# Heads of the second group computed inside their own stream, the sample tile's top-k first, a sixth slot for u rows

## The chip, the cores and the metric

The kernel runs on one core of a Trainium2 chip. The metric is the device time of one launch in microseconds; lower is better. The engines are PE (TensorE, matrix products), DVE (VectorE), ACT (ScalarE), POOL (GpSimd, which here issues the gathers) and SP (SyncE, which issues the weight loads). 16 DMA engines serve the core.

## What is computed

Two layers of a decoder trunk for two request groups that share weights: a prompt of 512 rows and 8 sample sequences of 8 rows (64 rows). Cut to what matters here:

```python
x += MixerBlock(rmsnorm(x))        # w_in (1024 x 7168), short conv, spatial gate, w_a_out, w_b_out, w_mix_o
x += CrossAttn(rmsnorm(x), mem)    # 4 heads, 256 memory tokens (a cache of its own for each sample sequence)
h = rmsnorm(x)                     # PEER
q = h @ w_pq                       # 8 heads x 2 halves x 128
s = q @ sub_keys                   # per head two lists of 128 scores
s1, i1 = top_k(s[..., 0], 16); s2, i2 = top_k(s[..., 1], 16)
cand = s1[:, None] + s2[None, :]; top_s, pos = top_k(cand, 16)
idx = (i1 * 128 + i2)[pos]         # 8 x 16 = 128 experts for each row
g = softmax(top_s)
out = sum_e g_e * gelu(h . peer_u[idx_e]) * peer_v[idx_e]
```

Each expert row is 1024 float32. For 128 rows of x, one *pick* (one of the 128 expert places) needs a gather of 128 rows of `peer_u` and 128 rows of `peer_v`, 0.524 MB each.

## The kernel before

**Tiles, passes and steps.** The rows are five tiles: prompt tiles 0 to 3 of 128 rows and the sample tile 4 of 64 rows. They form two groups: tiles 0 and 1; tiles 2, 3 and 4. A *pass* p is one layer for one group; p = 0 and 2 are the first group, 1 and 3 the second. Each pass has a *trunk* (mixer, cross-attention, scores) and a *stream* (its picks). The sample tile has its heads folded to two halves of the partitions and needs 64 picks, so the streams have 256, 320, 256 and 320 picks: they begin at picks 0, 256, 576 and 832, and there are 1152 in all. The order of the whole program is counted in *steps*, one for each pick m: POOL issues the u gather of pick m and then the v gather of pick m - 8 (`LAG`), DVE forms the dot products of pick m, and the sum of pick m - 8 is added, either by DVE (`sum_up`) or by PE as a product with a diagonal matrix that ACT writes (`peer_to` of PE; the picks in `plan_sums`). A stretch of PE sums is closed by a `merge` on DVE.

**Rings.** u rows have `NU` = 5 slots and v rows `NV` = 5. POOL works in order: u(m) waits until the dot of m - `NU` is done, v(m) until the sum of m - `NV` is done. Weights come through three slots `W` of 2 MB, each reloaded by SP when PE has finished the unit in it.

**What runs beside what.** The trunk of pass p runs during the stream of pass p - 1. `places` gives each trunk job a step; PE starts no job before its step's sums, and ACT and DVE take a job's result only when they come to its step. Before the change the trunk of pass 1 stands at steps 40 to 200, then its queries and scores (`pq`, `sc`, eight heads) at 200 to 247, all ahead of its stream at 256; that of pass 3 at 586 to 776 and 776 to 823, ahead of 832. The trunk of pass 2 has its first part (`par` to `v`) at 266 to 336, the rest at 336 to 520 and the heads to 567.

**Top-k.** The first tile of a pass gets its top-k head group by head group (`top_group`, sizes 2, 2, 2, 1, 1 in passes 1 to 3 and 1, 1, 2, 2, 2 in pass 0), cut in nine pieces between which `breathe` lets the stream go on as far as the window of the group has steps. For the later tiles `top_k` does all heads at once inside the stream, in 18 pieces spread over `topk_window`. `turns_to` counts the finished ones, in the order in which POOL, ACT and DVE wait for them.

**Sums.** In pass 1's stream the first 72 picks are summed on PE, then DVE sums until the last 56 picks; in pass 3's stream two of three are summed on PE. In pass 3 the dots read the tile's rows from PSUM (`rows_in_psum`, filled by `copy_rows` on ACT), otherwise from the SBUF tile `T`.

```python
if p == 2 * DEPTH - 1:
    return step_base(p) + NSEL * (i - 1) + OVER, step_base(p) + NSEL * i - LATEST
if p % 2:
    return step_base(p) + (0, TILE1)[i - 1], step_base(p) + (TILE1, 2 * HEAD)[i - 1]
```

Of the kernel before, what the change touches and what calls it, by code (L numbers as in the profile page):

```python
# [23 lines left out]
P = 128  # L24
# [7 lines left out]
DEPTH, CW = 2, 3  # L32
# [10 lines left out]
GRP = 4  # L43
NU, NV = 5, 5
WRING = 4
# [7 lines left out]
OVER = 3  # L53
TILE1 = 54
LATEST = 20
SEGS = 9
DIAG_EARLY = 3
# [39 lines left out]
def topk_window(p, i):  # L97

    if p == 2 * DEPTH - 1:
        return step_base(p) + NSEL * (i - 1) + OVER, step_base(p) + NSEL * i - LATEST  # L100
    if p % 2:
        return step_base(p) + (0, TILE1)[i - 1], step_base(p) + (TILE1, 2 * HEAD)[i - 1]
    if p:
        return step_base(p) + OVER, step_base(p) + NSEL - LATEST
    return step_base(p) + FIRST, step_base(p) + FIRST + WIDE
# [5 lines left out]


def head_steps(p):

    return (FIRST + LAG, 2 * HEAD, 0, 0)[p]

# [67 lines left out]


def head_groups(p):

    sizes = (2, 2, 2, 1, 1) if p else (1, 1, 2, 2, 2)
    return [(sum(sizes[:k]), n) for k, n in enumerate(sizes)]
# [9 lines left out]
def places(p):  # L199
# [4 lines left out]
    if p == 0:  # L204
# [5 lines left out]
        return out  # L210
    begin, end = step_base(p - 1) + (FIRST if p == 1 else LAG + 2), step_base(p)
    if p % 2:
        stretches = [(0, late, begin, end - CLOSE)]
    else:
        stretches = [(0, early, begin, step_base(p - 1) + 2 * HEAD), (early, late, step_base(p - 1) + 2 * HEAD, end - CLOSE)]
    stretches.append((late, len(mine), end - CLOSE, end - OVER - 6))
    out = []
# [8 lines left out]
def plan_jobs():  # L226
# [7 lines left out]
    for p in range(2 * DEPTH):  # L234
# [3 lines left out]
        for k, (name, owner, width, cost) in enumerate(mine):  # L238
# [7 lines left out]
            else:  # L246
# [4 lines left out]
                summing = any(a <= place[k] + 2 and since <= b + 1 for a, b in held_by_sums) or name[1] in ("pq", "sc")  # L251
                top = 6 if held or summing else 8
                cursor += cursor % width
                if cursor + width > top:
                    cursor = 0
                at = cursor
# [64 lines left out]
def plan_sums():  # L321
# [10 lines left out]
    for p in range(2 * DEPTH):  # L332
# [8 lines left out]
        for i, (t, rows) in enumerate(GROUPS[p % 2]):  # L341
            end = at + tile_picks(rows)

            since = at + 4 if i else at
            share = 2 if i == len(GROUPS[p % 2]) - 1 else 3
            span(at, end, step_base(p) + end - b + LAG, lambda m: m % share and m >= since)
            at = end
# [3 lines left out]
def decoder_step(nc, A, O):  # L351
# [17 lines left out]
    with ExitStack() as ctx:  # L369
# [44 lines left out]
        pos = sb("pos", [P, PH, TOPK], U16)  # L414
        part_of = sb("part_of", [P, 2, PH, TOPK], U16)
        pair = sb("pair", [P, PH, 2, TOPK], U16)
        sel = sb("sel", [P, PH, TOPK])
        gsum = sb("gsum", [P, PH])
# [197 lines left out]
        def final_steps(t):  # L616

            last = step_base(2 * DEPTH - 1)
            if t < 2:
                return last + 2 * HEAD + 8 + 12 * t, last + 2 * HEAD + 12 + 12 * t  # L620
            end = last + sum(tile_picks(rows) for n, rows in GROUPS[1] if n <= t) + LAG
# [7 lines left out]
        def head_window(p, k):  # L629

            ends = [AHEAD[p, "sc", h + n - 1] for h, n in head_groups(p)] + [FIRST if p == 0 else step_base(p) - OVER]
            return ends[k], ends[k + 1]

        def turns_to(p, i, h=PH - 1):

            n = sum(PH + len(GROUPS[q % 2]) - 1 for q in range(p))
            return n + h + 1 if i == 0 else n + PH + i

# [457 lines left out]
        def _(act):  # L1096
# [41 lines left out]

            asides = [(topk_steps(p, i, topk_parts(p, i)[1]), gate_exp, (p, i)) for p in range(2 * DEPTH) for i in range(1, len(GROUPS[p % 2]))]
            asides += [(final_steps(t)[0], final_square, (t,)) for t in range(NTILE - 1)]  # L1140
            asides += [(step_base(2 * DEPTH - 1) + at, copy_rows, (i,)) for i, at in ((1, 16), (2, 2 * NSEL - LATEST + GRP))]
            asides.sort(key=lambda a: a[0])
# [60 lines left out]
            def trunk(p):  # L1203
# [120 lines left out]
                for h in range(PH):  # L1324
# [9 lines left out]
                    for k, (h0, some) in enumerate(head_groups(p)):  # L1334
                        if k and h == h0 + some - 1:
                            group_exps(p, k - 1)
                if p == 2 * DEPTH - 1:
                    copy_rows(0)
                k = len(head_groups(p)) - 1
# [15 lines left out]
        def _(dve):  # L1355
# [88 lines left out]

            asides, going = [(p, i) for p in range(2 * DEPTH) for i in range(1, len(GROUPS[p % 2]))], []

# [143 lines left out]
            def top_group(p, k):  # L1590
# [300 lines left out]
```

## Time and profile before

| | us |
|---|---|
| median of 3 runs | 4321.12 (4315.29 to 4326.33) |
| the profiled execution | 4322.15 |
| its span | 4320.3 |

| engine | busy us | share |
|---|---|---|
| PE | 3404.0 | 79% |
| DVE | 3008.0 | 70% |
| POOL | 2638.8 | 61% |
| ACT | 930.1 | 22% |

The profile has one execution. Its first u gather starts at 503 us, when pass 0 has its first expert numbers; from there a stretch of steps is found in the trace by counting u gathers. Busy shares are means over stages whose limits differ, so the stage's own row is read, not the whole. "DMA share" is the mean busy share of the 16 DMA engines; it reads up to 1.03 where they are full.

### The profile page before, as it was taken

To read this page: it belongs to the slowest core of one execution; us is meant where nothing else is said; L and a number is where in the kernel's file an instruction comes from. 1 tells how busy PE (TensorE), PEld (TensorE's weight loads), DVE (VectorE), ACT (ScalarE), POOL (GpSimd) and SP (SyncE) were. 2 spreads that over 40 slices of the span, in tenths; PEclk is the share of its full clock that TensorE was granted. 3 is DMA by queue.
4 is the path that set the end of the run, shared out by engine and by line. 5 is a ranking of instruction groups with operands and counts; after the bars stand their busy time and mean duration, and the time that the engine had idled before them with its cause. 6 is when DMAs were issued, how large, how long until landed. Compare 5 with 4: busy or idle time off the path is not lost.

```text
span 4320.3 us, 36550 instructions
## 1 busy us (share of the span) xinstructions
PE 3404.0 (79%) x11088; PEld 2044.9 (47%) x11088; DVE 3008.0 (70%) x5941; ACT 930.1 (22%) x2730; POOL 2638.8 (61%) x2318
## 2 busy tenths in 40 slices
PE   8999979998888778968756959998777866556655
PEld 6875645774645323756334525764544422222211
DVE  2101377967668876886878688987768877776676
ACT  1001231121322322112212321122312311221221
POOL 0000175665657677777667676676667677777775
PEclk9899999999989899979877989899888888888878
DMA  5335498989999999999999989999999899999998
GB/s 190 120 136 185 178 355 311 390 334 357 364 369 403 363 361 374 399 388 405 409 400 401 397 312 361 404 374 397 366 368 403 313 401 409 404 410 409 403 410 329
DMA packets 461419, 1518.69 MB, mean 352 GB/s; under 512 B 41124, under 2 KB 45540, under 8 KB 461224
## 3 DMA queue, kind: packets, MB, share of 16 engines
q0 software_dynamic: 331776, 1208.11, 72.3%
q1 hardware_dynamic: 129448, 308.25, 19.0%
q8 instruction: 90, 1.47, 0.1%
q14 instruction: 105, 0.86, 0.1%
HBM read 1508.97 MB, written 7.23 MB: 351 GB/s over the span
## 4 chain that ended last, share of the span: by engine, by line
DMA 20%; POOL 19%; PE 12%; DVE 11%; issue 9%; ACT 1%; DVEq 0%; ACTq 0%
DMA vrow<-in_peer_v_dram,idx 15%; POOL urow L801 10%; POOL vrow L801 9%; PE ps L858 5%; DMA urow<-in_peer_u_dram,idx 4%; PE ps L883 4%; PE ps L902 3%; DVE X L1412 3%; DVE urow L1396 2%; DVE ps L1412 1%; DVE RB L1515 0%; DVE RB L1743 0%; PE ps L1084 0%; DVE T L1662 0%; DVE RB L1511 0%
## 5 line engine op out<-in xcount | busy, mean ns | idle before, releaser
L801 POOL DMA_INDIRECT urow<-in_peer_u_dram,idx x1152 | 1343.0, 1166 | 1192.5 <-DVE idx L1521 499.9
L801 POOL DMA_INDIRECT vrow<-in_peer_v_dram,idx x1152 | 1293.6, 1123 | 468.6 <-issue 305.6
L858 PE MATMUL ps<-vrow,diag 128*128 128x512 f32 x1804 | 993.0, 689 | 481.7 <-DMA vrow<-in_peer_v_dram,idx 460.2
L883 PE MATMUL ps<-RH,W 128*128 128x256 f32 (+1 forms) x4608 | 1169.4, 415 | 155.0 <-DVE RH L1676 61.1
L1396 DVE CUSTOM_DVE_ANT_0 urow<-urow,T 128x1024 f32<-128x1024 f32 x832 | 1015.8, 1223 | 312.5 <-DMA urow<-in_peer_u_dram,idx 280.5
L883 PEld LDWEIGHTS ps<-RH,W 128*128 128x128 f32 x4608 | 896.4, 195 | 429.9 <-DVE RH L1676 62.1
L858 PEld LDWEIGHTS ps<-vrow,diag 128*128 128x128 f32 x1804 | 360.8, 214 | 1067.2 <-issue 925.1
L1412 DVE SCALAR_TENSOR_TENSOR X<-vrow,wts,X 128x1024 f32<-128x1024 f32 x580 | 745.9, 1286 | 144.0 <-issue 130.3
L1396 DVE CUSTOM_DVE_ANT_0 urow<-urow,ps 128x1024 f32<-128x1024 f32 x320 | 389.1, 1220 | 211.9 <-DMA urow<-in_peer_u_dram,idx 207.2
L1165 ACT ACTIVATE gel<-dots 128x4 f32<-128x4 f32 x288 | 59.1, 205 | 2135.2 <-DVE dots L1396 2072.7
L902 PE MATMUL ps<-W,RB 128*128 128x512 f32 (+1 forms) x576 | 251.7, 597 | 7.1 <-ACT RB L1201 3.0
L883 PE MATMUL ps<-RB,W 128*128 128x256 f32 (+1 forms) x1024 | 251.5, 406 | 2.9 <-DVE RV L1777 1.5
L1167 ACT ACTIVATE wts<-gel,gate 128x1 f32<-128x1 f32 x1152 | 245.0, 283 | 9.3
L883 PEld LDWEIGHTS ps<-RB,W 128*128 128x128 f32 x1024 | 194.4, 190 | 57.3 <-DVE RV L1777 1.9
L902 PE MATMUL ps<-W,RV 128*128 128x512 f32 (+1 forms) x320 | 143.4, 608 | 42.7 <-DVE RV L1777 42.7
L1180 ACT ACTIVATE diag<-ident,wts 128x128 f32<-128x128 f32 x451 | 157.3, 390 | 89.7 <-PE ps L858 88.9
L902 PEld LDWEIGHTS ps<-W,RB 128*128 128x128 f32 (+1 forms) x576 | 105.6, 185 | 150.0 <-issue 140.3
L1412 DVE SCALAR_TENSOR_TENSOR ps<-vrow,wts,ps 128x1024 f32<-128x1024 f32 x115 | 148.2, 1289 | 15.1 <-DMA vrow<-in_peer_v_dram,idx 4.3
L902 PE MATMUL ps<-W,RH 128*128 128x512 f32 (+1 forms) x320 | 144.6, 605 | 15.6 <-DVE RH L1676 15.6
L1201 ACT ACTIVATE RB<-ps 128x256 f32<-128x256 f32 (+3 forms) x134 | 53.8, 419 | 312.5 <-PE ps L883 260.8
L902 PEld LDWEIGHTS ps<-W,RV 128*128 128x128 f32 (+1 forms) x320 | 58.1, 184 | 126.4 <-issue 81.9
L1201 ACT ACTIVATE RV<-ps 128x256 f32<-128x256 f32 (+3 forms) x106 | 48.8, 465 | 283.2 <-PE ps L883 267.8
(240 smaller groups left out, 2305.4 us busy)
## 6 DMA issues: line engine op xcount, KB each, us to landing
W<-in_w_in_dram SPq DMA_DIRECT2D x56, 2048.0 KB, 17.8
W<-in_w_pq_dram SPq DMA_DIRECT2D x16, 2048.0 KB, 19.1
urow<-in_peer_u_dram,idx POOLq DMA_INDIRECT x1152, 9.2
vrow<-in_peer_v_dram,idx POOLq DMA_INDIRECT x1152, 9.2
W<-in_w_a_out_dram SPq DMA_DIRECT2D x8, 2048.0 KB, 18.1
W<-in_w_b_out_dram SPq DMA_DIRECT2D x8, 2048.0 KB, 18.9
W<-in_w_mix_o_dram SPq DMA_DIRECT2D x8, 2048.0 KB, 14.5
W<-in_w_xq_dram SPq DMA_DIRECT2D x8, 2048.0 KB, 15.4
```

Source lines behind the costliest of these rows:

```text
L801: return pool.indirect_dma_start(ring[:, slot, :], None, table, bass.IndirectOffsetOnAxis(ap=idx[:, q % TSLOT, e:e + 1], axis=0))
L858: o = pe.matmul(ps[:, bank + b, :], diag[:, pe_turn[m] % NDIAG, :], vrow[:, m % NV, b * 512:(b + 1) * 512], start=m in pe_first, stop=m in ...
L883: m = pe.matmul(pf(name), slot(u)[:, k, c % BLK * P:c % BLK * P + P], src[:, k, 0:ncols(name[0] % 2)], start=(k == 0), stop=(k == KC - 1))
L902: m = pe.matmul(ps[0:rows, BANK[p, kind, i] + a, :], src[:, k, i * P:i * P + rows], row_slot((p, kind, n))[:, k % 4, a * 512:(a + 1) * 512 ...
L1165: ch.link(act.activation(gel[:, :], dots[:, at, :], ACT.Gelu_apprx_tanh))
L1167: w = act.activation(wts[:, at, j:j + 1], gel[:, j:j + 1], ACT.Copy, scale=gate[:, q % TSLOT, e + j:e + j + 1])
L1180: act.activation(diag[:, pe_turn[m] % NDIAG, :], ident[:, :], ACT.Copy, scale=wts[:, m // GRP % WRING, m % GRP:m % GRP + 1]).then_inc(diag ...
L1201: act.activation(out, in_, func).then_inc(act_evac, 1)
L1396: dve.tensor_tensor_reduce(urow[:, m % NU, :], urow[:, m % NU, :], rows, 1.0, 0.0, ALU.mult, ALU.add, dots[:, n % WRING, m % GRP:m % GRP + ...
L1412: dve.scalar_tensor_tensor(out=out, in0=vrow[:, m % NV, :], scalar=wts[:, m // GRP % WRING, m % GRP:m % GRP + 1], in1=base, op0=ALU.mult, ...
```

## The change

Seven things are changed together.

1. The u ring has six slots. To make room, `part_of` and `sel` are no longer tiles of their own but lie in `m16`.
2. In passes 1 and 3 (`carries`) the eight heads of the first tile are scored at steps -26, -14, -6, 2, 12, 22, 33 and 44 from the stream's begin (`CARRIED`), so five of them inside the stream that uses them, in groups 1, 1, 2, 2, 2. The trunk ahead of them ends at step 227 and 803 instead of 200 and 776.
3. All 128 picks of the first tile of these passes are summed on PE.
4. The later tiles' top-k of pass 1 stand at steps 322 to 350 (the sample tile, now first) and 350 to 378 (tile 3's rows); before at 256 to 310 and 310 to 336 in the other order. In pass 3 tile 3's top-k stands at 898 to 952 instead of 835 to 940.
5. The trunk of pass 2 begins at step 321; its first part ends at 350, the rest at 520 as before.
6. A head group's gates are normalised (`weigh_group`) after the first piece of the next group instead of after its last.
7. In pass 3 trunk jobs after step 818 leave PSUM banks 0 and 1 free, and the copies of rows for the dots, and the final norms of tiles 0 and 1, are placed anew.

```diff
-NU, NV = 5, 5
+NU, NV = 6, 5
-TILE1 = 54
+SAMPLE = 94
+CARRIED = (-26, -14, -6, 2, 12, 22, 33, 44)
+CARRY = 64
 def topk_window(p, i):
     if p == 2 * DEPTH - 1:
-        return step_base(p) + NSEL * (i - 1) + OVER, step_base(p) + NSEL * i - LATEST
+        return step_base(p) + (CARRY + 2 if i == 1 else NSEL * (i - 1) + OVER), step_base(p) + NSEL * i - (8 if i == 1 else LATEST)
     if p % 2:
-        return step_base(p) + (0, TILE1)[i - 1], step_base(p) + (TILE1, 2 * HEAD)[i - 1]
+        return step_base(p) + (SAMPLE, CARRY + 2)[i - 1], step_base(p) + (NSEL - 6, SAMPLE)[i - 1]
+def later_tiles(p):
+    return (2, 1) if p == 1 else tuple(range(1, len(GROUPS[p % 2])))
 def head_steps(p):
-    return (FIRST + LAG, 2 * HEAD, 0, 0)[p]
+    return (FIRST + LAG, NSEL + LAG, 0, NSEL + LAG)[p]
+def carries(p):
+    return p % 2 == 1
 def head_groups(p):
-    sizes = (2, 2, 2, 1, 1) if p else (1, 1, 2, 2, 2)
+    sizes = (1, 1, 2, 2, 2) if p == 0 or carries(p) else (2, 2, 2, 1, 1)
 # places
-    begin, end = step_base(p - 1) + (FIRST if p == 1 else LAG + 2), step_base(p)
+    begin, end = step_base(p - 1) + (FIRST if p == 1 else CARRY + 1 if p % 2 == 0 else LAG + 2), step_base(p)
     if p % 2:
-        stretches = [(0, late, begin, end - CLOSE)]
+        stretches = [(0, late, begin, end + CARRIED[0] - OVER if carries(p) else end - CLOSE)]
     else:
-        stretches = [(0, early, begin, step_base(p - 1) + 2 * HEAD), (early, late, step_base(p - 1) + 2 * HEAD, end - CLOSE)]
-    stretches.append((late, len(mine), end - CLOSE, end - OVER - 6))
+        stretches = [(0, early, begin, step_base(p - 1) + SAMPLE), (early, late, step_base(p - 1) + SAMPLE, end - CLOSE)]
+    if carries(p):
+        first = late
+        for h in range(PH):
+            after = [k for k, j in enumerate(mine) if j[0] == ("sc", h)][0] + 1
+            stretches.append((first, after, end + (CARRIED[h - 1] if h else CARRIED[0] - OVER), end + CARRIED[h]))
+            first = after
+    else:
+        stretches.append((late, len(mine), end - CLOSE, end - OVER - 6))
 # plan_sums, pass 3
-            span(at, end, step_base(p) + end - b + LAG, lambda m: m % share and m >= since)
+            span(at, end, step_base(p) + end - b + LAG, lambda m: m < b + head or m % share and m >= since)
 # top_group
                 each(lists, lambda a: dve.max_index(i16[:, a, 0:8], m16[:, a, 0:8], part[a]))
                 breathe()
+                if k:
+                    weigh_group(p, k - 1)
...
                 expert_ids(marks, h, n, idx[:, kept, where], layer_of(p)).then_inc(idx_done, n)
                 breathe()
-                if k:
-                    weigh_group(p, k - 1)
```

How the instructions move is shown at two places. The first is PE where the trunk of pass 2 comes to its first blocks of `w_in` (steps 337 and 351). A sum of one pick is `ps<-vrow,diag 128x512 x2`; a trunk job is `ps<-RH,W 128x256 x8`. Before:

```order
L858 MATMUL ps<-vrow,diag 128x512 x6
L902 MATMUL ps<-W,RH 128x512 x10
L858 MATMUL ps<-vrow,diag 128x512 x28
L883 MATMUL ps<-RH,W 128x256 x32
L914 MATMUL ps<-GV,ident 128x128 x16
L883 MATMUL ps<-RH,W 128x256 x224
```

And now:

```order
L923 MATMUL ps<-W,RH 128x512 x10
L879 MATMUL ps<-vrow,diag 128x512 x12
L904 MATMUL ps<-RH,W 128x256 x8
L879 MATMUL ps<-vrow,diag 128x512 x2
L904 MATMUL ps<-RH,W 128x256 x8
L879 MATMUL ps<-vrow,diag 128x512 x4
L904 MATMUL ps<-RH,W 128x256 x8
L879 MATMUL ps<-vrow,diag 128x512 x2
L904 MATMUL ps<-RH,W 128x256 x8
```

Before, PE had these 32 jobs to itself while DVE summed; now one or two sums of tile 2's picks stand behind every job until step 392.

The second place is DVE in a late head group of pass 3. Dots are `urow,dots<-urow,...`; MAX, MAX_INDEX and MATCH_REPLACE are the top-k. Before, one of the single-head groups ahead of step 832:

```order
L1614 MAX m<-RB 128x8 x2
L1615 MAX_INDEX i<-m,RB 128x8 x2
L1396 ISA urow,dots<-urow,T 128x1024
L1396 ISA dots 128x1
L1617 MATCH_REPLACE RB<-m,RB 128x128 x2
L1618 MAX m<-RB 128x8 x2
L1620 MAX_INDEX i<-m,RB 128x8 x2
L1481 TENSOR_TENSOR RB<-m 128x64
L1484 TENSOR_TENSOR RB<-m 128x48
L1396 ISA urow,dots<-urow,T 128x1024
```

And now, a group of two heads inside the stream:

```order
L1633 MAX m<-RB 128x8 x4
L1634 MAX_INDEX i<-m,RB 128x8 x4
L1415 ISA urow,dots<-urow,ps 128x1024
L1415 ISA dots 128x1
L1415 ISA urow,dots<-urow,ps 128x1024
L1415 ISA dots 128x1
L1605 RECIPROCAL ginv<-gsum 128x2
L1607 TENSOR_TENSOR gate<-gate,ginv 128x32
L1638 MATCH_REPLACE RB<-m,RB 128x128 x4
L1639 MAX m<-RB 128x8 x4
L1415 ISA urow,dots<-urow,ps 128x1024
```

Two or three dots now stand between pieces of a group where one or none stood, and the rows of the dot come from PSUM.

## Rows read from the trace of the kernel before

**Rows 1.** Section 2 and the DMA total of the profile's page.
```profile
GB/s 190 120 136 185 178 355 311 390 334 357 364 369 403 363 361 374 399 388 405 409 400 401 397 312 361 404 374 397 366 368 403 313 401 409 404 410 409 403 410 329
DMA packets 461419, 1518.69 MB, mean 352 GB/s; under 512 B 41124, under 2 KB 45540, under 8 KB 461224
```

**Rows 2.** Busy time by stretch: start:end, length, engines (instructions), clock, DMA share, GB/s.
```profile
core 0: us, PE busy (x) PEld busy (x) DVE busy (x) ACT busy (x) POOL busy (x), PEclk, DMA share, GB/s
626.00:891.00 265.00, 258.30 (x885) 164.37 (x884) 226.82 (x540) 45.47 (x128) 159.12 (x129) 0.92 0.91 335
891.00:1377.00 486.00, 420.97 (x1581) 266.25 (x1580) 342.86 (x495) 123.11 (x307) 306.69 (x246) 0.93 0.97 372
1377.00:1476.00 99.00, 83.28 (x265) 46.52 (x264) 85.09 (x284) 32.26 (x98) 65.96 (x60) 0.94 0.98 375
1476.00:1603.00 127.00, 92.64 (x203) 35.92 (x202) 92.75 (x296) 33.87 (x113) 100.17 (x89) 0.94 0.98 362
1603.00:1760.00 157.00, 137.12 (x390) 71.84 (x389) 116.50 (x266) 35.67 (x108) 117.50 (x101) 0.95 0.99 376
1760.00:1903.00 143.00, 105.34 (x429) 85.85 (x427) 119.64 (x173) 14.69 (x67) 110.29 (x84) 0.83 1.03 403
1903.00:2521.00 618.00, 444.74 (x1573) 298.90 (x1574) 480.15 (x846) 152.31 (x432) 436.29 (x368) 0.86 1.02 397
2521.00:2635.00 114.00, 75.09 (x196) 32.04 (x195) 86.61 (x180) 22.10 (x67) 89.56 (x66) 0.85 0.83 297
2635.00:3048.00 413.00, 376.34 (x1326) 252.99 (x1325) 357.76 (x642) 77.49 (x204) 278.24 (x220) 0.90 1.00 386
3048.00:3352.00 304.00, 237.74 (x939) 149.49 (x938) 225.45 (x334) 79.32 (x214) 201.07 (x169) 0.89 0.99 385
3352.00:3453.00 101.00, 88.03 (x275) 48.86 (x274) 86.86 (x292) 35.28 (x106) 68.67 (x61) 0.88 0.88 311
3453.00:3577.00 124.00, 76.55 (x131) 26.67 (x130) 91.94 (x212) 26.05 (x101) 93.91 (x97) 0.88 1.02 400
...
503.00:4320.00 3817.00, 2928.39 (x9236) 1693.61 (x9234) 2932.08 (x5771) 870.68 (x2615) 2636.59 (x2304) 0.89 0.98 379
```

**Rows 3.** Three of the same stretches, u gathers on POOL alone: their count gives the steps.
```profile
626.00:891.00 265.00, 82.68 (x65) 0.92 0.91 335
...
1760.00:1903.00 143.00, 57.26 (x42) 0.83 1.03 403
...
2635.00:3048.00 413.00, 151.49 (x110) 0.90 1.00 386
```

**Rows 4.** Stretches again, the sums on PE alone (four instructions a pick): PE, PEld, clock, DMA.
```profile
1300.00:1377.00 77.00, 19.76 (x42) 7.76 (x43) 0.93 1.03 401
...
1476.00:1603.00 127.00, 86.83 (x170) 31.60 (x169) 0.94 0.98 362
...
3453.00:3577.00 124.00, 76.55 (x131) 26.67 (x130) 0.88 1.02 400
```

**Rows 5.** Groups of POOL from 1476 to 1603 us: count, busy, mean ns, idle before.
```profile
L801 POOL DMA_INDIRECT vrow<-in_peer_v_dram,idx x44 | 54.6, 1240 | 13.4 <-issue 7.6 <-PE ps L858 5.8
L801 POOL DMA_INDIRECT urow<-in_peer_u_dram,idx x45 | 46.4, 1031 | 13.7 <-issue 13.7
```

**Rows 6.** POOL's waits (total, times, longest) from 626 to 1300 us, then from 1903 to 2521 us.
```profile
POOL urow L801 <- DVE dots L1396: 167.0, 60, 10.6
...
POOL urow L801 <- DVE dots L1396: 46.6, 25, 6.8
```

**Rows 7.** GB/s in 40 slices from 3395 to 3453 us.
```profile
GB/s 325 271 384 398 418 393 401 407 410 415 396 412 379 136 268 136 381 373 297 314 342 288 381 277 381 133 3 82 308 237 102 17 206 322 206 184 220 345 376 297
```

**Rows 8.** DVE on tile `KV`, tile 3's top-k, from 1476 to 1663 us.
```profile
1476.00:1663.00 187.00, 40.82 (x202) 0.94 0.97 359
```

**Rows 9.** Section 5 of the page: a dot and a sum on DVE.
```profile
L1396 DVE CUSTOM_DVE_ANT_0 urow<-urow,T 128x1024 f32<-128x1024 f32 x832 | 1015.8, 1223 | 312.5 <-DMA urow<-in_peer_u_dram,idx 280.5
...
L1412 DVE SCALAR_TENSOR_TENSOR X<-vrow,wts,X 128x1024 f32<-128x1024 f32 x580 | 745.9, 1286 | 144.0 <-issue 130.3
```

More of the change, by code:

```diff
@@ L252, in plan_jobs @@
                 top = 6 if held or summing else 8
+                low = 2 if p == 2 * DEPTH - 1 and place[k] > step_base(p) + CARRIED[1] else 0
                 cursor += cursor % width
-                if cursor + width > top:
-                    cursor = 0
+                if cursor < low or cursor + width > top:
+                    cursor = low
                 at = cursor
@@ L414, in decoder_step @@
         pos = sb("pos", [P, PH, TOPK], U16)
-        part_of = sb("part_of", [P, 2, PH, TOPK], U16)
         pair = sb("pair", [P, PH, 2, TOPK], U16)
-        sel = sb("sel", [P, PH, TOPK])
         gsum = sb("gsum", [P, PH])
@@ L442, in decoder_step @@
         qT, oT = F1, F2
+        spent = m16[:, :, :].rearrange("p (h i) n -> p h i n", i=2)
+        sel = spent[:, :, 1, :]
+        part_of = m16[:, :, :].bitcast(U16).rearrange("p (h i) n -> p h i n", i=2)[:, :, 0, :].rearrange("p h (j n) -> p h j n", j=2)
         S = [RB[:, 0:2 * DM], KV[:, 0:2 * DM], RB[:, 2 * DM:3 * DM]]
@@ L619, in final_steps @@
             if t < 2:
-                return last + 2 * HEAD + 8 + 12 * t, last + 2 * HEAD + 12 + 12 * t
+                return last + NSEL - 4 + 8 * t, last + NSEL + 8 * t
             end = last + sum(tile_picks(rows) for n, rows in GROUPS[1] if n <= t) + LAG
@@ L629, in head_window @@
         def head_window(p, k):
-            ends = [AHEAD[p, "sc", h + n - 1] for h, n in head_groups(p)] + [FIRST if p == 0 else step_base(p) - OVER]
+            ends = [AHEAD[p, "sc", h + n - 1] for h, n in head_groups(p)] + [FIRST if p == 0 else step_base(p) + CARRY if carries(p) else step_base(p) - OVER]
             return ends[k], ends[k + 1]
@@ L636, in turns_to @@
             n = sum(PH + len(GROUPS[q % 2]) - 1 for q in range(p))
-            return n + h + 1 if i == 0 else n + PH + i
+            return n + h + 1 if i == 0 else n + PH + later_tiles(p).index(i) + 1
         def sum_step(m):
@@ L1137, in group_exps @@
                     head_exp(p, h)
-            asides = [(topk_steps(p, i, topk_parts(p, i)[1]), gate_exp, (p, i)) for p in range(2 * DEPTH) for i in range(1, len(GROUPS[p % 2]))]
+            asides = [(topk_steps(p, i, topk_parts(p, i)[1]), gate_exp, (p, i)) for p in range(2 * DEPTH) for i in later_tiles(p)]
             asides += [(final_steps(t)[0], final_square, (t,)) for t in range(NTILE - 1)]
-            asides += [(step_base(2 * DEPTH - 1) + at, copy_rows, (i,)) for i, at in ((1, 16), (2, 2 * NSEL - LATEST + GRP))]
+            asides += [(step_base(2 * DEPTH - 1) + at, copy_rows, (i,)) for i, at in ((0, -8), (1, CARRY + 8), (2, 2 * NSEL - LATEST + GRP))]
             asides.sort(key=lambda a: a[0])
@@ L1336, in trunk @@
                             group_exps(p, k - 1)
-                if p == 2 * DEPTH - 1:
-                    copy_rows(0)
                 k = len(head_groups(p)) - 1
@@ L1443, in final_tile @@
                                          in1=last_g[0:rows, :], op0=ALU.mult, op1=ALU.mult).then_inc(y_done, 1)
-            asides, going = [(p, i) for p in range(2 * DEPTH) for i in range(1, len(GROUPS[p % 2]))], []
+            asides, going = [(p, i) for p in range(2 * DEPTH) for i in later_tiles(p)], []
             def aside_to(n):
@@ L1490, in split_places @@
                 place = pos[:, h:h + nh, :]
-                by_wide, by_narrow = part_of[:, 0, h:h + nh, :], part_of[:, 1, h:h + nh, :]
+                by_wide, by_narrow = part_of[:, h:h + nh, 0, :], part_of[:, h:h + nh, 1, :]
                 row, col = pair[:, h:h + nh, 0, :], pair[:, h:h + nh, 1, :]
```

## The prediction

> **What bounds the kernel now.** I read the slices of the page first [rows 1]. After about the fifth slice the DMA engines are nearly full: the stream that no trunk disturbs holds 403 to 410 GB/s, and I take 409 GB/s as what this core can draw. Then I split the span by steps [rows 2], counting u gathers [rows 3]. From the first gather at 503 us to the end are 3817 us at 379 GB/s, so 1447 MB. At 409 GB/s they need 3537 us. The change moves no byte less, so **280 us is all that it can win**, and the question is in which stretches this loss lies. Loss is the length less GB/s times length over 409:
>
> - steps 0 to 40: 11 of 123, in the slices of the page.
> - steps 40 to 104 (626 to 891 us): 265 - 217 = 48. PE is busy 258 of 265 us and DVE 227.
> - steps 104 to 227 (to 1377): 486 - 442 = 44.
> - steps 227 to 256 (to 1476): 99 - 91 = 8.
> - steps 256 to 350 (to 1760): 284 - 257 = 27. There POOL hardly waits; its gathers last 1.03 and 1.24 us and 0.3 us lie between two [rows 5], so a step costs POOL 2.8 to 2.9 us, and hardly a weight is loaded that could use what is left of the DMA engines.
> - steps 350 to 576 (to 2521): 761 - 741 = 20.
> - steps 576 to 608 (to 2635): 114 - 83 = 31, the same picture.
> - steps 608 to 718 and 718 to 802 (to 3352): 23 and 18.
> - steps 802 to 832 (to 3453): 101 - 77 = 24. The fine slices fall to 3 and 17 GB/s [rows 7]: single-head groups with one to six steps to spread over.
> - the rest: 3 to step 880, and some 24 behind it, most of it the drain at the end.
>
> So the DMA engines bound the kernel, except where PE, DVE and POOL together can't feed them.
>
> **The change part by part.** One pick moves 1.05 MB, so 2.56 us at 409 GB/s. The sum is made against the profiled execution (4322.15 us; the median of the runs shown is 4321.12, 1 us less).
>
> *Steps 40 to 104.* The trunk ahead of the heads is spread over 187 steps instead of 160, so these 64 steps hold 34% of it instead of 40%. Of PE's 258 us, about 20 are the last ten sums of pass 0's first 40 picks at 1.9 us [rows 4]; the other 238 shrink to about 204, 224 with the sums. DVE keeps its dots, sums and the top-k of tile 1 and falls to about 219. The DMA engines need 217 less a seventh of 22 MB of weights (8 us), 209. With the margin that such a balance has now (265 over 258, with DVE at 227) I take 245: **-20**, bounds -35 and -5.
>
> *Steps 104 to 227.* They hold 66% of that trunk, where before they held 60% and the first half of the queries. The bytes stay (442 us), PE goes from 421 to about 410, DVE from 343 to 349. Nothing is removed; what goes is the cluster of queries, heads and their sums at the end and the density of the attention part, where DVE stands behind PE's jobs in order and POOL behind DVE: 167 us of waits for dots from 626 to 1300 [rows 6]. I take a loss of 19 instead of 44: **-25**, bounds -40 and 0.
>
> *Steps 227 to 256.* Three heads instead of six, two weight units (4 MB, 10 us) later: 99 to 90, **-9**, bounds -15 and 0.
>
> *Steps 256 to 350.* Five heads come in: 10 query jobs, about 45 us of PE with their scores. PE's sums cost 19.8 us for 10.5 picks to 86.8 us for 42.5, 1.9 to 2.0 us each [rows 4]; heads and sums together are 2.9 us a step over 44 steps, no more than POOL's 2.8 to 2.9. The 4 MB of weights fit in what the DMA engines have left. DVE loses the whole top-k of tile 3 and gains the heads. What is late next is POOL, as before: **0**, bounds -10 and +10.
>
> *Steps 350 to 392.* Here the change costs. Before, these 42 steps took 143 us, PE busy 105 of them without a sum [rows 2]. Now the trunk of pass 2 has 170 steps instead of 184 (105 becomes 113) and 42 sums are added. At 1.9 us these are 80: 193 us of PE against 143. The row's clock is 0.83 and rises to 0.95 and more where PE has no pause, so part of the 113 shrinks, down to 98; the DVE sums that PE takes over (1.29 us each [rows 9]) were not the limit. 178 to 193 against 143: **+40**, bounds +20 and +57. The moved weights come in behind: **+11**. The top-k of tile 3 in 28 steps is 41 us on DVE [rows 8] beside 34 of dots (28 at 1.22 us [rows 9]) and some 10 of trunk (119.6 us in the row of 42 steps, less 42 dots and 43 sums at 1.29 us), under PE's 28 x 4.4. It ends at 378, six steps ahead of its first gather, and may hold POOL for a few microseconds.
>
> *Steps 392 to 576 and 576 to 608.* Trunk 8% denser where the DMA engines are full (397 GB/s) and PE is idle a quarter: 0. The begin of pass 3's trunk lies as before: 0.
>
> *Steps 608 to 718.* Pass 3's trunk is spread over 217 steps instead of 190. The jobs that filled 608 to 701 now reach to 718: 17 steps more of picks for the same PE work (about 326 of the 376 us), DVE 347, the DMA engines 370. I take 388 for 413: **-25**, bounds -35 and -5. *Steps 718 to 802*: no step is freed, 0. *Steps 802 to 832*: three groups with ten-step windows instead of five in 36 steps; POOL at 2.9 and some weights give 92 for 101: **-9**, bounds -20 and 0.
>
> *Steps 832 to 880.* Five heads (45 us of PE) join the stream, and all picks are summed on PE, 48 at 1.9 to 2.3 us [rows 4]. 136 us of PE for 124 before, where the DMA engines were full: **+12**, bounds +3 and +30. Behind it PE has room for every sum.
>
> *The sixth u slot.* POOL works in order and v keeps five slots. v(n-8) waits for the sum of n-13, which DVE makes right behind dot n-5. So where DVE sums, the sixth slot gives one dot (1.2 us) of slack, not a step; where PE sums it gives a whole gather. Most waits for dots lie where the DMA engines are full (46.6 us from 1903 to 2521 [rows 6], at 397 GB/s) and are worth nothing. **-10**, bounds -30 and 0. The earlier gates, the aliased tiles and the moved copies: 0, since ACT is idle three quarters of the time and the gates come more than ten steps ahead of their picks.
>
> Sum: -20 - 25 - 9 + 0 + 40 + 11 - 25 - 9 + 12 - 10 = **-35 us, 4287 us**.
>
> One rule speaks against all of it. The rows show 403 to 410 GB/s for hundreds of microseconds. The Trainium skill, page DMA: Bandwidth & Descriptors, section Specifications, gives about 358 GB/s as the limit of HBM for one core. By it the stretches at 372 to 410 GB/s would be at or over the limit already and the sum would be near 0, at 4322 us. The trace does not agree: the mean after the first gather is 379. I give that rule no chance of its own.
>
> **The rivals.**
>
> *The jobs' own chain, not their density, sets steps 104 to 227 and 608 to 718.* Each trunk job waits for an evacuation and that for DVE's or ACT's place in the order; if this takes its time however many steps lie between, both -25 become -5, and the sum is +5: **4327 us**, no change. For it: PE is busy only 87% of 891 to 1377. Against it: spread jobs leave more steps between them for dots, and DVE's waits there cost gathers.
>
> *PE becomes the wall in the second streams (slower).* The 98 more picks on PE, beside trunk jobs, at the dear end of each row: 57 for 40 in steps 350 to 392, 7 for 0 ahead of it (2.04 us a sum), 36 for 12 from 832 (2.34 us a sum), and no use of the slot since v slots stay taken while PE is late: +58, **4345 us**. It decides as soon as a sum beside a trunk job costs over 2 us, because then the step is over 4.6 us where the DMA engines need 3.5. For it: 2.04 and 2.34 us are rows. Against it: these contain waits for rows that have not landed, which go when PE is late; PE's 19.8 us for 10.5 sums lie in a stretch at 401 GB/s.
>
> *Slack is what was missing.* If one gather more in the ring and looser heads let POOL run through the bursts, the slot gives 30 and PE's place costs 20: -75, **4247 us**. For it: POOL waited 60 times from 626 to 1300 us, 2.8 us on average, about one step. Against it: the v ring.
>
> *The slot does nothing*, the v ring alone decides: 4297 us, inside the forecast.
>
> **How the numbers follow.** Forecast with the idle slot in it 0.46, chain 0.20, PE wall 0.12, slack 0.22. A measurement of this kernel can tell about 0.3% or 13 us from no change. Faster: 0.22 + 0.46 (less 0.04 for its upper edge) + a bit of the chain, 0.68; slower: 0.12; same: 0.20. The range reaches from 4235, a little beyond the slack case, to 4332, beyond the chain case; it leaves out most of the PE wall and what lies below.
>
> **What would show it.** Steps 40 to 104 in about 245 us and 104 to 227 in about 461; 350 to 392 in about 183 instead of 143, PE full and the DMA share under 0.9; no slices under 100 GB/s ahead of step 832; 832 to 880 in about 136. u waits for dots fall, v waits for PE rise. The forecast is wrong if 104 to 227 stays at 486, if PE's stretch from 350 lasts 200 or only 150, or if a new wait of POOL for expert numbers appears at steps 288 to 384.

## The result: 0.36% slower, and where the 13 us lie

| | us |
|---|---|
| changed kernel, median of 14 runs | 4337.52 (4332.21 to 4347.30) |
| kernel before, 14 runs beside them | 4325.22 (4315.29 to 4334.43) |
| ratio | 1.0036, 95% interval 1.0028 to 1.0044 |
| span of the profiled execution, before and after | 4320.3 and 4333.3 |

The forecast was 4287 us with a range of 4235 to 4332. The change is slower, by a little, where it was called faster.

The page of the changed kernel, mean GB/s in 40 slices and the busy times:

```profile
PE 3518.1 (81%) x11480; PEld 2098.7 (48%) x11480; DVE 2888.1 (67%) x5843; ACT 973.2 (22%) x2833; POOL 2589.2 (60%) x2318
GB/s 186 126 134 183 187 359 359 384 361 402 376 374 304 374 371 358 358 342 403 400 408 402 406 312 363 391 385 406 376 358 342 369 387 409 396 411 409 409 408 330
```

Against [rows 1] the slices from the sixth to the twelfth are better in all but one (384 against 390 in the eighth). Then 304 stands where 403 stood, three slices around 1.8 ms have fallen (from 374, 399 and 388 to 358, 358 and 342), and near 3.3 ms 403 has become 342. DVE works 120 us less than before, PE 114 us more: the work moved as planned.

The same stretches as [rows 2], cut again by counting u gathers, for the changed kernel:

```profile
core 0: us, PE busy (x) PEld busy (x) DVE busy (x) ACT busy (x) POOL busy (x), PEclk, DMA share, GB/s
622.00:863.00 241.00, 227.13 (x793) 142.64 (x792) 221.68 (x528) 38.47 (x121) 147.00 (x128) 0.95 0.98 366
863.00:1234.00 371.00, 308.35 (x1163) 205.98 (x1164) 282.80 (x373) 100.23 (x235) 248.19 (x194) 0.89 0.98 376
1234.00:1343.00 109.00, 99.78 (x316) 48.58 (x316) 53.87 (x71) 19.12 (x52) 56.13 (x53) 0.94 0.88 332
1343.00:1449.00 106.00, 89.42 (x286) 51.81 (x287) 62.40 (x150) 27.07 (x89) 66.38 (x60) 0.94 0.95 362
1449.00:1735.00 286.00, 239.03 (x625) 111.50 (x624) 185.67 (x526) 86.00 (x266) 206.97 (x188) 0.97 0.97 363
1735.00:1907.00 172.00, 170.71 (x639) 118.50 (x638) 112.51 (x349) 34.86 (x112) 90.81 (x85) 1.00 0.95 352
...
2644.00:3035.00 391.00, 345.09 (x1207) 235.04 (x1206) 344.76 (x627) 71.35 (x193) 274.25 (x221) 0.90 1.02 394
3035.00:3255.00 220.00, 142.57 (x595) 93.88 (x594) 170.49 (x217) 56.74 (x148) 149.88 (x118) 0.82 0.95 367
3255.00:3363.00 108.00, 92.18 (x282) 43.96 (x281) 53.54 (x70) 20.05 (x57) 56.81 (x51) 0.92 0.88 342
3363.00:3461.00 98.00, 91.95 (x297) 53.26 (x296) 63.98 (x151) 27.93 (x90) 65.16 (x61) 0.96 0.96 368
3461.00:3589.00 128.00, 118.71 (x353) 61.38 (x352) 87.74 (x246) 42.88 (x136) 93.06 (x96) 1.00 1.01 388
```

Put side by side, in us; "e1" is the first experiment below:

| steps | before | forecast | changed | e1 |
|---|---|---|---|---|
| 0 to 40 | 123 | 123 | 119 | 119 |
| 40 to 104 | 265 | 245 | 241 | 242 |
| 104 to 201 | 409 | | 371 | 373 |
| 201 to 227 | 77 | | **109** | 89 |
| 104 to 227 together | 486 | 461 | 480 | 462 |
| 227 to 256 | 99 | 90 | 106 | 93 |
| 256 to 350 | 284 | 284 | 286 | 287 |
| 350 to 392 | 143 | 183 to 194 | 172 | 172 |
| 392 to 608 | 732 | 732 | 737 | 736 |
| 608 to 718 | 413 | 388 | 391 | 390 |
| 718 to 777 | 227 | | 220 | 220 |
| 777 to 802 | 77 | | **108** | 87 |
| 718 to 802 together | 304 | 304 | 328 | 307 |
| 802 to 832 | 101 | 92 | 98 | 98 |
| 832 to 880 | 124 | 136 | 128 | 127 |
| 880 to the end | 743 | 743 | 744 | 743 |

The gains of the spread trunk are there: 24 us in steps 40 to 104, 38 in 104 to 201 and 22 in 608 to 718. They are eaten by three places: steps 201 to 227 and 777 to 802, 32 and 31 us longer and the same place in two passes, which the forecast did not have; and steps 350 to 392, 29 us longer, which it had.

What happens in the first of them can be read from PE's instructions in order of time, in the changed kernel. `L923` from `W,RB` is the xo product (the attention's output projection), `L879` are sums, four instructions each:

```profile
1272.97 6.32 PE L923 MATMUL ps<-W,RB 128*128 128x512 f32 x8 [0.88 <-ACT RB L1222]
1280.23 1.95 PE L879 MATMUL ps<-vrow,diag 128*128 128x512 f32 x4 [0.94 <-DMA vrow<-in_peer_v_dram,idx]
1282.02 3.60 PE L923 MATMUL ps<-W,RB 128*128 128x512 f32 x8
1285.45 1.88 PE L879 MATMUL ps<-vrow,diag 128*128 128x512 f32 x4
...
1310.17 1.88 PE L879 MATMUL ps<-vrow,diag 128*128 128x512 f32 x4
1311.89 17.47 PE L923 MATMUL ps<-W,RB 128*128 128x512 f32 x40
1329.29 5.42 PE L879 MATMUL ps<-vrow,diag 128*128 128x512 f32 x12
```

POOL's waits in this stretch (total, times, longest) are:

```profile
POOL vrow L822 <- PE ps L879: 31.4, 7, 14.6
POOL vrow L822 <- DVE X L1431: 15.0, 5, 6.2
```

The xo product takes 42 us of PE where it stands alone (e1 below). It fell on steps 185 to 195 before, and now falls on 209 to 221. The span of PE sums that closes pass 0's stream begins at pick 201, so at step 209, in both kernels; PE makes three of four sums there, DVE the fourth. Before, the product had ended when PE began to sum; now PE sums while it makes the product, at first one sum for every 3.6 to 7.2 us of product and at the end none for 17.5 us. The v slots stay full, and POOL, which works in order, then issues neither v nor u gathers. Of its 31.4 us of waits for PE the block of 17.5 us accounts for one of 14.6; six shorter ones make the other 16.8.

PE is also simply full there. From its first sum to the three sums behind the block it has no pause, while the DMA share is 0.75:

```profile
1280.00:1334.50 54.50, 54.27 (x124) 21.43 (x125) 21.60 (x30) 10.13 (x30) 19.46 (x20) 1.00 0.75 278
```

The product over its 12 steps is 3.5 us a step, and three of four sums at 1.88 us add 1.4: about 4.9 us a step (an estimate), where a pick needs 2.56 us of the DMA engines. In the second stretch (3255 to 3363 us) it is not quite the same: PE stands still for 8.28 us ahead of its first sum, for a v row that has not landed, with most of the product behind that sum in its queue.

### The profile page after: what moved, and what is told of

Read it like the earlier page. It is cut to its first block, busy times and chain, and to the rows that moved or that the text cites. A ratio compares the mean times of both kernels' runs of the same rounds, so it can differ in the third digit from the quotient of the medians.

```text
span 4333.3 us, 37457 instructions
## 1 busy us (share of the span) xinstructions
PE 3518.1 (81%) x11480; PEld 2098.7 (48%) x11480; DVE 2888.1 (67%) x5843; ACT 973.2 (22%) x2833; POOL 2589.2 (60%) x2318
## 4 chain that ended last, share of the span: by engine, by line
PE 38%; DMA 22%; POOL 18%; DVE 11%; issue 8%; ACT 1%; SPq 0%; DVEq 0%; ACTq 0%; POOLq 0%
DMA vrow<-in_peer_v_dram,idx 17%; PE ps L904 17%; PE ps L879 10%; POOL vrow L822 10%; PE ps L923 9%; POOL urow L822 8%; DMA urow<-in_peer_u_dram,idx 4%; DVE X L1431 3%; DVE urow L1415 2%; PE ps L893 1%; PE ps L1105 1%; PE ps L1068 0%; DMA RH<-in_sg_w_dram 0%; DVE KV L1530 0%; DVE ps L1431 0%
## 5 line engine op out<-in xcount | busy, mean ns | idle before, releaser
L822 POOL DMA_INDIRECT vrow<-in_peer_v_dram,idx x1152 | 1328.2, 1153 | 856.8 <-DVE X L1431 319.4
L822 POOL DMA_INDIRECT urow<-in_peer_u_dram,idx x1152 | 1258.8, 1093 | 866.9 <-DVE idx L1540 499.6
L879 PE MATMUL ps<-vrow,diag 128*128 128x512 f32 x2196 | 1116.6, 644 | 396.0 <-DMA vrow<-in_peer_v_dram,idx 363.4
L879 PEld LDWEIGHTS ps<-vrow,diag 128*128 128x128 f32 x2196 | 416.4, 202 | 1020.3 <-issue 872.2
L1431 DVE SCALAR_TENSOR_TENSOR X<-vrow,wts,X 128x1024 f32<-128x1024 f32 x524 | 673.0, 1284 | 152.7 <-issue 129.5
L923 PE MATMUL ps<-W,RB 128*128 128x512 f32 (+1 forms) x576 | 257.6, 606 | 8.4 <-DVE RB L1813 4.4
L1201 ACT ACTIVATE diag<-ident,wts 128x128 f32<-128x128 f32 x549 | 198.2, 392 | 248.4 <-PE ps L879 247.3
L923 PE MATMUL ps<-W,RV 128*128 128x512 f32 (+1 forms) x320 | 144.4, 612 | 54.3 <-DVE RV L1796 54.3
L923 PEld LDWEIGHTS ps<-W,RB 128*128 128x128 f32 (+1 forms) x576 | 107.0, 188 | 155.0 <-issue 144.0
L923 PE MATMUL ps<-W,RH 128*128 128x512 f32 (+1 forms) x320 | 143.0, 600 | 19.5 <-DVE RH L1695 19.5
L923 PEld LDWEIGHTS ps<-W,RV 128*128 128x128 f32 (+1 forms) x320 | 58.4, 185 | 138.6 <-issue 82.5
L923 PEld LDWEIGHTS ps<-W,RH 128*128 128x128 f32 (+1 forms) x320 | 57.2, 181 | 101.0 <-issue 80.2
L1431 DVE SCALAR_TENSOR_TENSOR ps<-vrow,wts,ps 128x1024 f32<-128x1024 f32 x75 | 96.6, 1288 | 10.0 <-DMA vrow<-in_peer_v_dram,idx 4.1
```

The source lines that it names most:

```text
L822: return pool.indirect_dma_start(ring[:, slot, :], None, table, bass.IndirectOffsetOnAxis(ap=idx[:, q % TSLOT, e:e + 1], axis=0))
L879: o = pe.matmul(ps[:, bank + b, :], diag[:, pe_turn[m] % NDIAG, :], vrow[:, m % NV, b * 512:(b + 1) * 512], start=m in pe_first, stop=m in ...
L923: m = pe.matmul(ps[0:rows, BANK[p, kind, i] + a, :], src[:, k, i * P:i * P + rows], row_slot((p, kind, n))[:, k % 4, a * 512:(a + 1) * 512 ...
L1201: act.activation(diag[:, pe_turn[m] % NDIAG, :], ident[:, :], ACT.Copy, scale=wts[:, m // GRP % WRING, m % GRP:m % GRP + 1]).then_inc(diag ...
L1431: dve.scalar_tensor_tensor(out=out, in0=vrow[:, m % NV, :], scalar=wts[:, m // GRP % WRING, m % GRP:m % GRP + 1], in1=base, op0=ALU.mult, ...
```

## Theory and rivals for the experiments

A: the closing PE sums now stand beside the xo product in PE's queue. That can cost in two ways, and no run here keeps one and removes the other: the order (sums held behind product, the 17.5 us block) and the load (sums and product together are more than PE can do in these steps). B: attention and xo take their time wherever they lie, and only the place moved. C: the rings (a sixth u slot that gives nothing, or harms). For 350 to 392: PE's sums against DVE's load. The first four kernels ran on one chip with 13 runs of the kernel before (4320.94 us), the next three on a second (19 runs, 4324.71 us), the last two on a third; so ratios to before are compared, and stretches.

## e1: the closing PE sums begin behind the xo product

```diff
+TAIL = 32
 # plan_sums
-            span(b + n - CLOSE, b + n, ...)
+            close = CLOSE if p % 2 else TAIL
+            span(b + n - close, b + n, ...)
```

> The changed kernel, but the PE sums that close pass 0's and pass 2's streams begin at the last 32 picks (225 and 801) instead of the last 56 (201 and 777). Theory A: the time was lost in steps 201 to 227 and 777 to 802 (109 and 108 us against 78 and 77 before), because the xo product, which PE now makes at steps 209 to 221, stands in PE's order ahead of sums, so v slots stay full and POOL waits for v. Then DVE sums there free the slots: 201 to 227 falls from 109 to 80 to 90 us, 777 to 802 from 108 to 80 to 90, the whole to 4280 to 4305. Rival B: these steps are longer because attention and xo now fall into them, whoever sums: 201 to 227 stays over 100 us and the time within 10 us of 4337. Rival C: it was DVE's lost slack from another place, the ring of six: same as B here.

Measured: 4282.20 us, ratio 0.9899 (0.9874 to 0.9924). Against the changed kernel's 1.0036 that is 1.4% or 59 us from one number (55 by the medians, 52 by the two profiled spans). Steps 201 to 227, 227 to 256 and 777 to 802:

```profile
1239.00:1328.00 89.00, 78.81 (x265) 39.56 (x264) 62.94 (x79) 14.91 (x38) 57.40 (x52) 0.92 1.01 396
1328.00:1421.00 93.00, 78.25 (x264) 48.16 (x265) 70.22 (x153) 25.02 (x83) 68.38 (x58) 0.93 1.02 398
...
3226.00:3313.00 87.00, 72.12 (x240) 36.00 (x239) 63.23 (x78) 15.97 (x43) 58.33 (x51) 0.91 1.03 407
```

PE makes the product in one piece, and POOL's waits are short ones for DVE (PE's product, then the waits of 1239 to 1328 us):

```profile
1277.75 42.21 PE L925 MATMUL ps<-W,RB 128*128 128x512 f32 x94
...
POOL vrow L824 <- DVE X L1433: 18.1, 8, 4.0
```

The edit covers 24 picks in each pass; six of them DVE summed already, so DVE takes 18 sums more. With DVE at 54 of 109 us in the changed kernel it had the room. The DMA share rises from 0.88 to 1.01. A holds and B falls: attention and xo lie where they lay. By the table every stretch but these three is the changed kernel's to 2 us. That 227 to 256 falls from 106 to 93 is probably the lateness that it had inherited; seven of the 18 moved sums fall into it by the count of instructions.

PE's busy time falls with the length, from 99.78 to 78.81 us while the stretch goes from 109 to 89, so e1 shows that sums beside the product cost the time, and not whether it is their order or PE's load.

## e2: the same loss made in the kernel before

```diff
+TAIL = 86
-            span(b + n - CLOSE, b + n, ...)
+            close = CLOSE if p % 2 else TAIL
+            span(b + n - close, b + n, ...)
```

> The kernel before, but its closing PE sums of passes 0 and 2 begin 30 picks earlier (picks 170 and 746), so that they are on PE while it makes the xo product at steps 185 to 195 and 758 to 770. Theory A: the same loss appears in the old kernel, 15 to 30 us in each of the two passes, with v waits for PE of over 10 us beside the xo product: 4350 to 4385. Rival B: no difference beyond 10 us.

Measured: 4360.37 us, ratio 1.0084 (1.0062 to 1.0107), 36 us slower. Steps 178 to 201 and 756 to 777, first in the kernel before and then in e2:

```profile
1211.00:1300.00 89.00, 81.52 (x286) 42.45 (x284) 59.17 (x72) 15.94 (x39) 49.25 (x48) 0.93 1.02 397
...
3195.00:3275.00 80.00, 68.13 (x238) 34.86 (x236) 56.17 (x67) 16.84 (x40) 45.73 (x42) 0.94 1.03 406
```

```profile
1207.00:1313.00 106.00, 102.00 (x326) 48.73 (x324) 41.45 (x58) 20.43 (x54) 50.72 (x46) 0.98 0.83 317
...
3211.00:3306.00 95.00, 88.57 (x273) 40.86 (x271) 39.85 (x55) 20.13 (x53) 46.60 (x43) 1.00 0.88 340
```

and POOL's wait in the first, with its block on PE:

```profile
POOL vrow L803 <- PE ps L860: 44.2, 9, 17.0
...
1278.80 17.47 PE L904 MATMUL ps<-W,RB 128*128 128x512 f32 x40
```

The loss is 17 and 15 us in these two stretches and 8 and 3 in those behind them (85 and 80 us against 77 and 77), with the same 17.5 us block. Without the moved heads, the slot or anything else of the change, the overlap alone makes the loss. Here too PE's busy time grows by as much as the time (81.52 to 102.00 and 68.13 to 88.57 us).

## e3 and e7: which ring

e3 gives the changed kernel five u slots (`NU, NV = 5, 5`), e7 gives the sixth slot to v (`NU, NV = 5, 6`).

> The changed kernel with five u slots instead of six. From the waits (u waits of POOL for dots went from 411 us to under 60, v waits from 162 to 610, with the sum of waits where the DMA engines are not full hardly less) I expect the slot to be worth 5 to 15 us: 4342 to 4352. If the slot does nothing because the v ring is next: 4337 within 5. If the slot itself harms (earlier u gathers ahead of v gathers): 4325 to 4332.

> The changed kernel with the sixth slot given to v instead of u (NU 5, NV 6). If PE's xo block holds v slots, one more v slot lets one more pair of gathers out in each block: steps 201 to 227 and 777 to 802 fall from 109 and 108 to 100 to 105, and against the kernel with five slots in both rings (4356.6) the whole falls by 5 to 25: 4330 to 4352. If the block is long against any slot (17.5 us of product, 2.6 us for a pick), less than 5 us in the two stretches together.

Measured: e3 4356.57 us, ratio 1.0069 (1.0046 to 1.0092); e7 4320.64 us, ratio 0.9990 (0.9978 to 1.0002). By ratios the u slot is worth 0.33% (14 us, the ends of the two intervals leave 0.02% to 0.64%), the v slot 0.79% (34 us). Both expectations missed the time: e3 is slower than its 4342 to 4352, e7 faster than its 4330 to 4352. POOL's waits over the whole span, first of the changed kernel, then of e3:

```profile
POOL vrow L822 <- DVE X L1431: 319.4, 150, 10.6
POOL vrow L822 <- PE ps L879: 290.8, 208, 15.3
...
POOL urow L822 <- DVE dots L1415: 29.6, 57, 3.9
```

```profile
POOL urow L822 <- DVE dots L1415: 325.6, 225, 10.6
...
POOL vrow L822 <- PE ps L879: 251.7, 196, 15.3
POOL vrow L822 <- DVE X L1431: 71.4, 49, 1.9
```

With the sixth u slot 296 us of u waits become 248 us more of v waits for DVE and 39 more for PE: the v ring is next, as the prediction said, and most of the wait only changes its name. Beside the xo product no slot helps: steps 201 to 227 last 110 us in e3, 109 in the changed kernel and 108 in e7, 777 to 802 last 109, 108 and 106. In the first of them POOL's longest wait for PE is 11.7, 14.6 and 9.2 us in these three, and the length does not follow it; PE is busy for 99.8 to 100.8 us in all three. That speaks for the load. e7's gain lies in 227 to 256 and 256 to 350:

```profile
1351.00:1441.00 90.00, 83.16 (x280) 49.38 (x279) 56.35 (x140) 25.04 (x82) 65.54 (x58) 0.98 0.98 383
1441.00:1715.00 274.00, 229.73 (x605) 106.35 (x605) 182.61 (x514) 85.23 (x267) 209.60 (x188) 0.98 1.00 384
```

They last 106 and 286 us in the changed kernel; 350 to 392 gives 7 us back (179 against 172). The prediction called 256 to 350 bound by POOL. That was not the whole: with one v slot more it goes 12 us faster at nearly the same POOL time (209.60 us here, 206.97 there). POOL waited 30.6 us for PE's sums in the changed kernel and 13.3 us here, so part of its loss was v slots waiting for PE.

## e4: fewer PE sums ahead of step 392

```diff
-    return (FIRST + LAG, NSEL + LAG, 0, NSEL + LAG)[p]
+    return (FIRST + LAG, 92 + LAG, 0, NSEL + LAG)[p]
```

> The changed kernel, but in pass 1's stream only the first 92 picks of tile 2 are summed on PE (before the change 72, in the changed kernel 128); DVE sums from pick 348. PE had no pause in steps 350 to 392 (172 us, before 143). If PE's sums are the price there, the stretch falls to 150 to 160 us, the whole to 4320 to 4328. If DVE is as full there, with the top-k of tile 3 in steps 350 to 378, it stays at 165 to 185 us and the time at 4335 or above.

Measured: 4324.57 us, ratio 1.0005 (0.9992 to 1.0018), 0.31% or 13 us under the changed kernel. Steps 350 to 392 and 392 to 448:

```profile
1735.00:1903.00 168.00, 148.59 (x608) 116.89 (x606) 150.97 (x383) 22.83 (x76) 94.01 (x85) 0.94 0.99 374
1903.00:2093.00 190.00, 130.95 (x554) 110.28 (x554) 148.40 (x200) 41.73 (x106) 141.96 (x113) 0.81 1.02 400
```

The first compares with 172 us and PE at 170.71 in the changed kernel: PE is let go (148.59 of 168), and DVE takes its place (150.97, from 112.51). 4 us of 29 come back there. The other 9 to 10 come behind it: 392 to 448 falls from about 200 to 190 (193 before the change). The expectation had two branches and each is half met: the stretch stays over 165 us, the time lies in 4320 to 4328. POOL's waits in the first stretch say what is next, first in the changed kernel and then in e4:

```profile
POOL vrow L822 <- PE ps L879: 71.7, 30, 7.5
```

```profile
POOL vrow L822 <- DVE X L1431: 47.2, 22, 6.7
POOL vrow L822 <- PE ps L879: 9.2, 5, 3.0
```

So PE's sums were the limit in 350 to 392, and with 36 of them taken from PE, DVE's sums are. DVE has 39.6 us of work on tile 3's top-k there, which stood at 256 to 310 before; that this is what makes its sums late fits, but was not tried alone.

One caution for reading single stretches: e4's edit acts only from step 356 on, yet its profile has 377 us for 104 to 201 and 98 for 227 to 256, where the changed kernel has 371 and 106. A stretch of a single profile can differ by 6 to 8 us with nothing changed in it.

## e5, e8, e9: the edits together

e5 has both edits (e1's and e4's) and six u slots, e8 the same with `NU, NV = 5, 6`, e9 is e5 with `TAIL = 44`.

> The changed kernel with both edits: closing PE sums of passes 0 and 2 only from picks 225 and 801, and in pass 1's stream PE sums for 92 picks instead of 128. If the two causes are apart (v slots held beside xo; PE without a pause behind step 350) their effects add: 4282 less 10 to 14, so 4266 to 4275. If the second only moves a wait that the first removed as well: 4278 to 4285.

> The kernel with both edits (4277 us), the sixth slot with v instead of u. In the changed kernel the v slot beat the u slot by 17 us, but hardly in the two stretches of the xo block (108 and 106 against 109 and 108): it gained in 256 to 350 (274 against 287) and 227 to 256. Those stretches are left in this kernel too, so if the gain is of PE sums and single holes there: 4260 to 4268. If it stood in for the held slots: 4275 or above.

> The kernel with both edits and six u slots (4277 us), but the closing PE sums begin at picks 213 and 789, so at step 221, the first behind the xo product (steps 209 to 221), not at 233. If the xo block alone is the cause, the sums beside the transposes and the norm behind it cost nothing: 201 to 227 stays at 86 to 92 us and the time within 5 us of 4277. If every sum ahead of the queries costs: 201 to 227 at 95 to 105, the time 4285 to 4300.

Measured: e5 4277.13 us, ratio 0.9892 (0.9875 to 0.9908); e8 0.9918 (0.9893 to 0.9944); e9 0.9897 (0.9857 to 0.9937). e8 and e9 ran on a chip on which the kernel before took 4445.61 us, and they took 4412.55 and 4399.33 us.

- e5 has the lowest ratio here, 1.1% under the kernel before. Whether e4's edit adds to e1's is not settled by the ratios (0.9892 and 0.9899, with intervals over both), and its 4277 us lie between the two cases that were expected. The stretches speak for it: 167 us for 350 to 392 and 191 for 392 to 448, e1 172 and 200, and each pair is found again in other profiles (168 and 190 in e4 and e9, 173 and 200 in e3).
- e9 begins the sums at step 221, right behind the product. Its 201 to 227 and 777 to 802:

```profile
1251.00:1340.00 89.00, 82.65 (x277) 40.94 (x278) 62.85 (x79) 16.28 (x43) 57.98 (x52) 0.95 1.01 395
...
3244.00:3330.00 86.00, 73.74 (x240) 37.17 (x239) 62.52 (x76) 17.56 (x48) 57.25 (x51) 0.91 1.03 407
```

  As in e5 (89 and 87). Sums beside the norm and its transposes cost nothing that shows; those beside the product did.
- e8 is not shown to be better or worse than e5 or e9. The v slot, which beat the u slot by 0.46% in the changed kernel, gives no such gain here. Why stays open: in 227 to 256 it still does (88 us, e9 on the same chip 95), and other stretches are longer than e9's (440 us against 429 for 448 to 576).

## e6: the sixth u slot in the kernel before

The only edits to the kernel before are `NU, NV = 6, 5` and the aliased tiles.

> The kernel before with six u slots and the aliased tiles, nothing else. In the changed kernel the slot was worth 19 us (4356.6 against 4337.5). The prediction gave it 10 with bounds 0 and 30 by waits of the kernel before: 4305 to 4315 if it is worth the same here, 4318 to 4324 if it only helps the new order.

Measured: 4314.48 us, ratio 0.9977 (0.9967 to 0.9986): 10 us, the forecast's figure for this part, and all of it independent of the moved heads.

## Why the prediction was wrong, step by step

- **The ceiling** (280 us to win, DMA engines at 409 GB/s): it held. No slice of the changed kernel's page went over 411.
- **Steps 40 to 104, -20:** right, -24.
- **Steps 104 to 227, -25:** this is the step that failed. Its jobs were costed as busy time of PE, DVE and the DMA engines over all 123 steps, and that sum came out right: PE was forecast at about 410 us and is busy for 408. But 100 of these lie in the 109 us of the last 26 steps. Neither the load of PE in those steps nor the order of its queue was looked at. The text said that "nothing is removed; what goes is the cluster"; but something was moved past something: the xo product past step 209, where PE takes over the sums. So the steps took 480 us for the 461 forecast. The expected 461 us are there once the sums begin later (462 in e1). How the loss divides between load and order stays open. The fence of rows in the part on the change looked at pass 2's first block, where single jobs have sums between them, and not at xo, where 40 instructions stand in a row.
- **Steps 227 to 256, -9:** +7, gone with the same edit; 93 us in e1 for the 90 forecast.
- **Steps 718 to 802, 0:** +24, the same cause a second time; 307 in e1 for 304.
- **Steps 608 to 718, -25:** right, -22.
- **Steps 256 to 350, 0:** right in size (+2), wrong in cause: POOL did not bound it alone, see e7.
- **Steps 350 to 392, +40 and +11:** +29. Right in kind: PE is busy for 170.71 of 172 us at clock 1.00. Its sums cost 1.84 us each there (76.31 us for 166 instructions), the forecast's 1.9; the trunk has 94 us left, less than the 98 to 113 taken. The rising clock is not shown to be the reason: the `w_in` products (128x256) took 0.23 us of busy time each in both kernels (83.4 us for 365 at clock 0.83, 99.8 us for 441 at 1.00). The 11 us for moved weights did not come on top of PE's time. The DMA share was expected under 0.9 and is 0.95. DVE's load was called no bound, and e4 shows its sums as the next one.
- **Steps 802 to 832, -9:** -3, in e1 also -3. The slices under 100 GB/s are not gone in the changed kernel: in 40 slices from 3363 to 3421 us there are three, at 57, 37 and 76. In e1 they are gone: of 40 slices from 3311 to 3411 us none is under 298. Still the stretch lasts 98 us there too, and which wait sets that was not looked into.
- **Steps 832 to 880, +12:** +4. PE is at 118.71 of 128 us for the 136 that were forecast. Its sums cost 1.82 us each (82.99 us for 182 instructions; 1.9 forecast, 2.34 in the row of before), and 36 us are left for the heads that were taken at 45.
- **The sixth slot, -10:** right, 10 us in the kernel before, 14 in the changed one. Over the whole span POOL's u waits for dots fell from 411.4 to 29.6 us and its v waits for PE rose from 97.3 to 290.8, as it said; those for DVE rose from 64.5 to 319.4.

Of the rivals, "PE becomes the wall" named the engine and the ring that were to blame ("v slots stay taken while PE is late"), but put them at steps 256 to 392 and from 832, with the condition that a sum costs over 2 us. That the measured 4337.5 us lies near its 4345 is chance (and by its own price of 2.34 us its third term is 33, not 36). Sums cost 1.82 to 1.88 us. What decided was what stands beside them: with the xo product a step of PE takes about 4.9 us even so, and its queue has a stretch of 17.5 us without a sum. The chain rival (each -25 becomes -5) is refuted: in e1 the two are -24 and -23. The kernel without the overlap, e1, takes 4282 us, 5 us from the 4287 forecast; that is partly luck, since errors cancel (the pieces from 350 to 392 and 832 to 880 were too dear by 22 and 9, those of 227 to 256, 392 to 608 and 802 to 832 too cheap by 3 to 6 each).

## What to carry to other kernels

When work that was summed or fed by one in-order engine is shifted along a schedule, list what it crosses on that engine's queue, and add the busy times over the few steps in which the two meet, not over a stage: PE was busy for 408 of 480 us in steps 104 to 227, and for 100 of 109 in the last 26 of them. A ring of five slots at 2.6 us a pick covers about 13 us (an estimate), less than a block of 17.5 us. When a kernel has a table of who does what from which step on, every entry belongs to the placement of the jobs around it, and moving the jobs means moving the entry; here that one number was worth 52 to 59 us, over four times the measured loss. Then read the longest gap between two consumers of the ring from the engine's order of time.

## What the runs showed of the hardware

The granted clock of PE was 1.00, which is 2.4 GHz throughout, where PE had no pause (1735 to 1907 us, PE busy 170.71 of 172), and 0.83 in the same steps before [rows 2]. But it was 1.00 too in steps 880 to 960, where PE was busy for 157 of 211 us:

```profile
3589.00:3800.00 211.00, 157.09 (x323) 54.41 (x321) 149.48 (x440) 60.05 (x202) 157.28 (x160) 1.00 1.02 402
```

In these steps before the change the clock was 0.88 with PE busy for 127.45 of 209 us. That added PE work paid for a part of itself by the clock is not shown.

On the third chip the last stream, which has no trunk beside it, ran at 362 GB/s with the same work of POOL as elsewhere (steps 960 to the end of e8; the changed kernel on its own chip has 533 us at 393 GB/s there):

```profile
3829.00:4408.00 579.00, 322.02 (x496) 110.77 (x495) 369.02 (x601) 109.00 (x390) 372.51 (x392) 0.79 0.94 362
```

The kernel before lost 120 us on that chip too. The absolute times did not stay, so this document compares ratios; why that chip feeds less was not tried and stays open.
